# Shared expert's rows kept in SBUF and added in the last stage of a one-core encoder layer

## The reference

```
idx, wts = route(h2, w_router, router_bias)
shared = (jax.nn.silu(h2 @ w_sg) * (h2 @ w_su)) @ w_sd
ffn = routed_experts(h2, idx, wts, w_eg, w_eu, w_ed) + shared
x = layer_norm(ALPHA * x + ffn.reshape(B, T, D_MODEL), ln2_g, ln2_b)
```

## Time and profile before

| what | us |
|---|---|
| median of 3 runs | 2419.66 |
| lowest, highest run | 2417.68, 2421.93 |
| profiled execution, its own time | 2428.82 |
| its span, first to last instruction | 2426.9 |
| PE busy | 2284.9 (94%) |
| DVE busy | 1405.8 (58%) |
| ACT busy | 963.1 (40%) |
| POOL busy | 1496.5 (62%) |
| mean granted clock of TensorE | 0.987 |

### The profile page before, as it was taken

How to read it: one execution, slowest core, us unless ns; L and a number is a source line. 1 busy time by engine, 2 the same in 40 slices (tenths; PEclk the granted TensorE clock), 3 DMA queues, 4 the chain that set the end, 5 groups by cost and what they waited for, 6 DMA issues and landing times. The chain is left out here.

```text
span 2426.9 us, 40519 instructions
## 1 busy us (share of the span) xinstructions
PE 2284.9 (94%) x15460; PEld 2011.2 (83%) x15460; DVE 1405.8 (58%) x2749; ACT 963.1 (40%) x1582; POOL 1496.5 (62%) x1525
## 2 busy tenths in 40 slices
PE   4999999999999999999998999999999999999882
PEld 4889899898898998989987776578898888888882
DVE  7365665755756647557567697534455555555344
ACT  3452734526436346263364232122323333333334
POOL 6355674675646646657467256577667777776533
PEclk9999999999999999999998999999999999999996
DMA  5201112011011111111112641599999999999995
GB/s 181 77 28 45 41 45 60 29 44 50 29 45 49 46 50 37 36 50 37 47 38 78 194 133 47 154 281 300 310 348 350 354 352 350 351 352 360 363 353 181
DMA packets 210602, 380.72 MB, mean 157 GB/s; under 512 B 25810, under 2 KB 132558, under 8 KB 209898
## 3 DMA queue, kind: packets, MB, share of 16 engines
q1 hardware_dynamic: 180218, 302.25, 34.8%
q0 software_dynamic: 30192, 75.89, 13.1%
HBM read 310.71 MB, written 76.41 MB: 160 GB/s over the span
## 5 line engine op out<-in xcount | busy, mean ns | idle before, releaser
L128 PE MATMUL ps<-xTh,w_mix_low 128*128 128x368 f32 (+1 forms) x1728 | 594.1, 344 | 7.0 <-POOL w_mix_low L122 5.7
L130 PE MATMUL ps<-xTh,w_mix_high 128*128 128x368 f32 (+3 forms) x1808 | 598.9, 331 | 0.4 <-issue 0.4
L129 PE MATMUL ps<-xTl,w_mix_high 128*128 128x368 f32 (+3 forms) x1808 | 597.1, 330 | 1.5 <-issue 1.5
L2298 POOL DMA_INDIRECT xg_early<-h_d,tabq_early x304 | 313.2, 1030 | 153.8 <-issue 80.8
L129 PEld LDWEIGHTS ps<-xTl,w_mix_high 128*128 128x128 f32 (+1 forms) x1808 | 340.1, 188 | 15.8 <-issue 9.5
L128 PEld LDWEIGHTS ps<-xTh,w_mix_low 128*128 128x128 f32 x1728 | 329.3, 191 | 20.5 <-issue 15.4
L130 PEld LDWEIGHTS ps<-xTh,w_mix_high 128*128 128x128 f32 (+1 forms) x1808 | 339.4, 188 | 5.6 <-issue 1.8
L2310 POOL DMA_INDIRECT ys_d<-yo,tab_early x114 | 216.6, 1900 | 112.6 <-issue 50.6
L122 POOL TENSOR_TENSOR w_mix_low<-w_mix_raw,w_mix_high 128x1024 fp32r<-128x1024 f32 x72 | 182.7, 2537 | 120.9 <-ACT w_mix_high L117 83.1
L1333 POOL TENSOR_TENSOR x_m<-x_m,kh_m 128x128 f32<-128x128 f32 (+1 forms) x272 | 125.4, 461 | 114.6 <-ACT x_m L866 114.6
L2340 PEld LDWEIGHTS ps<-xgT,wg_early 128*128 128x128 f32 x1376 | 177.6, 190 | 19.3 <-issue 18.6
(11 more groups left out here) (396 smaller groups left out, 4558.8 us busy)
## 6 DMA issues: line engine op xcount, KB each, us to landing
wd_early<-in_w_exp_down SPq DMA_DIRECT2D x43, 1024.0 KB
wg_early<-in_w_exp_gate SPq DMA_DIRECT2D x82, 512.0 KB
wu_early<-in_w_exp_up SPq DMA_DIRECT2D x82, 512.0 KB
w_mix_raw<-in_w_in SPq DMA_DIRECT2D x72, 512.0 KB, 3.8
wg<-in_w_exp_gate SPq DMA_DIRECT2D x42, 512.0 KB
wu<-in_w_exp_up SPq DMA_DIRECT2D x42, 512.0 KB
wd<-in_w_exp_down SPq DMA_DIRECT2D x21, 1024.0 KB
xg_early<-h_d,tabq_early POOLq DMA_INDIRECT x316
```

Source lines behind the costliest of these rows:

```text
L128: pe.matmul(out, ll, rh, start=start, stop=False)
L129: pe.matmul(out, lh, rl, start=False, stop=False)
L130: return pe.matmul(out, lh, rh, start=False, stop=stop)
L2298: pool.indirect_dma_start(out=xg[:, b, g, :], out_offset=None, in_=h2_d[:, :].rearrange("t (q n) -> (t q) n", q=4), in_offset=bass.Indirec ...
```

## The change

The four buffers and the nine accumulating transfers go. All nine tiles of shared rows stay in one SBUF tensor, `shr`, to the end. To make room, tensors of the bridge that die early lie inside it: the shared expert's gate and up weights in tiles 2 to 5, gain and shift of the first norm in tiles 6 and 7, router weights and small tables in tile 8. `rows_out` waits for these users at tiles 6 and 8 (for tiles 2 to 5 the order of TensorE's queue does it). The planes of expert 62 lie in the dead second buffers of gate and up weights, expert 63 uses `wdh` and `wdl`. In the last stage each loaded tile first gets its shared rows added (a join), four on VectorE and five on GpSimd, and ScalarE's measures wait for GpSimd's joins. `last_norm` now loads into `yn`, which lies over buffers of the experts. The name `LATE`, defined twice before (65536, then 6), is split in two: `BEHIND` takes the second meaning and `LATE` keeps 65536 for rows past an expert's room.

```diff
@@ bridge
-        wg, wu, wd = sb("swg", [P, KT, FE]), sb("swu", [P, KT, FE]), sb("swd", [P, 2, D])
-        hT, sl, ys = sb("shT", [P, 2, T]), sb("ssl", [P, 2, 368]), sb("ys", [P, 2, D])
+        wd = sb("swd", [P, 2, D])
+        shr = sb("shr", [P, NT, D])
+        wg, wu = (shr[:, t:t + 2, :].rearrange("p t d -> p (t d)").rearrange("p (k n) -> p k n", k=KT) for t in (2, 4))
+        gcol, bcol = shr[:, 6, :], shr[:, 7, :]
+        wr, rb = shr[:, 8, 0:KT * NE].rearrange("p (k n) -> p k n", k=KT), shr[:, 8, KT * NE:(KT + 1) * NE]
+        hT, sl = sb("shT", [P, 2, T]), sb("ssl", [P, 2, 368])
...
                 act.wait_ge(d_done, 2 * t + b + 1)
-                if b == 0 and t == 2:
-                    act.wait_ge(m_low, NT - 1)
-                if b == 0 and t >= 4:
-                    act.wait_ge(y_out[t % 4], 16 * (t // 4))
-                act.activation(shared_rows(t)[:m, cols(b)], ps[:m, (G, U)[b], :], ACT.Copy, scale=1.0 / ALPHA).then_inc((y_left, y_right)[b], 1)
+                if b == 0 and t == 6:
+                    act.wait_ge(y_ready, NT)
+                if b == 0 and t == 8:
+                    act.wait_ge(routed, NT)
+                act.activation(shr[:m, t, cols(b)], ps[:m, (G, U)[b], :], ACT.Copy, scale=1.0 / ALPHA).then_inc((y_left, y_right)[b], 1)
...
-            def add_shared(t):
-                m = rows(t)
-                pool.wait_ge(y_left, t + 1)
-                pool.wait_ge(y_right, t + 1)
-                pool.wait_ge(stored[t % 2], 32 * (t // 2 + 1))
-                pool.dma_start(ys_d[t * P:t * P + m, :], shared_rows(t)[:m, :], accum_op=ALU.add).then_inc(y_out[t % 4], 16)
-
...
-            add_shared(0)
-            add_shared(1)
-            add_shared(2)
-            add_shared(3)
-            add_shared(4)
             gather(0)
-            add_shared(5)
             gather(1)
-            add_shared(6)
-            add_shared(7)
-            add_shared(8)
@@ experts
-            n = e - (NE - 2)
-            return (wdh[:, :, :], wdl[:, :, :]) if n < 0 else (last_planes[:, n, 0, :, :], last_planes[:, n, 1, :, :])
+            return (last_high[:, :, :], last_low[:, :, :]) if e == NE - 2 else (wdh[:, :, :], wdl[:, :, :])
...
-            for n in range(4):
-                pool.wait_ge(y_out[n], 16 * len(range(n, NT, 4)))
...
-                if e and e < NE - 2:
+                if e == NE - 2:
+                    act.wait_ge(u_done, e)
+                elif e == NE - 1:
+                    act.wait_ge(d_done, e - 1)
+                elif e:
                     act.wait_ge(d_done, e)
@@ last_norm, VectorE's measure, ScalarE's measure, GpSimd
             dve.wait_ge(y_in[t], 16)
+            dve.tensor_tensor(xr[:m, t, :], xr[:m, t, :], shr[:m, t, :], ALU.add).then_inc(joined, 1)
+            dve.wait_ge(joined, n + 1)
...
-            act.wait_ge(y_in[t], 16)
+            act.wait_ge(joined_pool, n + 1)
...
+        def join(t):
+            m = rows(t)
+            pool.wait_ge(y_in[t], 16)
+            pool.tensor_tensor(xr[:m, t, :], xr[:m, t, :], shr[:m, t, :], ALU.add).then_inc(joined_pool, 1)
+
+        join(MEASURED[0])
+        join(MEASURED[1])
         pool.wait_ge(rows_in, 32)
         for n, t in enumerate(BY_POOL):
             m = rows(t)
+            join(MEASURED[n + 2])
             pool.wait_ge(unit_ready, n + 1)
```

More of the change, by code:

```diff
@@ L180, in first_experts @@
                 ("tab", [P, NE, 2], U32), ("tabw", [P, NE, 2], F32), ("tb", [NE, CAP, 2], U32), ("tbf", [NE, CAP], F32),
-                ("twice", [NE, 2, LOW], F32), ("fourfold", [NE, 4, QUAD], F32), ("tabq", [P, GROUPS, NE], U32))]
+                ("twice", [NE, 2, LOW], F32), ("fourfold", [NE, 4, QUAD], F32), ("tabq", [P, GROUPS, NE], U32))[begin:]]
         constants(nc, ident, ones, before)
@@ L202, in build @@
             ns, nb, nl = (len(x.split()) for x in (SHARED_SEMAPHORES, BRIDGE_SEMAPHORES, LAST_SEMAPHORES))
-            bridge(nc, block, sems[:ns], sems[ns:ns + nb], a, ps, ident, ones, before, st, w_raw, w_high, late, woh, wol, mT_d, xn_d, h2_d, ys_d, tok_d, plan_d,
+            shr = bridge(nc, block, sems[:ns], sems[ns:ns + nb], a, ps, ident, ones, before, st, w_raw, w_high, late, woh, wol, mT_d, xn_d, h2_d, ys_d, tok_d, plan_d,
                    gates_d, only_d, dest_d, picks_d, pairs_d, step_d, limit_d, place, order, early)
@@ L206, in build @@
             c2 = ctx.enter_context(ExitStack())
-            first_experts(c2, "_reserved")
+            last_planes = []
+            for n in ("high", "low"):
+                c2.enter_context(nc.sbuf_tensor("first_of_two_" + n, [P, KT, FE], F32))
+                last_planes.append(c2.enter_context(nc.sbuf_tensor("last_" + n, [P, 2, D], F32R)))
+            first_experts(c2, "_reserved", 2)
             wg, wu, wd, xg, tab, tabw, tabq = early[:6] + early[-1:]
-            bufs = [wg, wu, wd, xg] + [c2.enter_context(nc.sbuf_tensor(n, shape, F32)) for n, shape in (
-                ("sl", [P, 2 * CAP]), ("yo", [P, 2, 2, D]))]
-            last, added = experts(nc, block, sems[:ns], sems[ns + nb:-nl], a, ps, ident, h2_d, ys_d, order, tab, tabw, tabq, bufs, c2)
+            bufs = [wg, wu, wd, xg]
+            last, added = experts(nc, block, sems[:ns], sems[ns + nb:-nl], a, ps, ident, h2_d, ys_d, order, tab, tabw, tabq, shr, last_planes, bufs, c2)
             last_norm(nc, block, sems[-nl:], a, o, ps, ys_d, added, *last)
@@ L1258, in _ @@
                 last_merge()
-                for k in range(EARLY, LATE):
+                for k in range(EARLY, BEHIND):
                     dve.wait_ge(wo_high, k + 1)
@@ L1443, in bridge @@
         only = sb("only", [P, NE])
-        fill = sb("fill", [P, 2 * FILL], U32)
+        fill = shr[:, 8, (KT + 2) * NE:(KT + 2) * NE + 2 * FILL].bitcast(U32)
         tokens = sb("tokens", [P, NT], U32)
@@ L1553, in first_tile @@
                 for k in range(FIRST, HEADS):
-                    if k >= LATE:
-                        pe.wait_ge(wo_low, k - LATE + 1)
+                    if k >= BEHIND:
+                        pe.wait_ge(wo_low, k - BEHIND + 1)
                     for b in range(2):
@@ L1910, in tables @@
                     dve.tensor_copy(tabw[:, some, j], ps[:, RB, n * NE:(n + 1) * NE][:, some]).then_inc(tab_s, 1)
-            for k in range(LATE, HEADS):
-                split_low(dve, wol[:, k, :], late[k - LATE], woh[:, k, :]).then_inc(wo_low, 1)
+            for k in range(BEHIND, HEADS):
+                split_low(dve, wol[:, k, :], late[k - BEHIND], woh[:, k, :]).then_inc(wo_low, 1)
             dve.wait_ge(first_high, 1)
@@ L2184, in _, with experts @@
             send(8)
-            add_shared(0)
-            add_shared(1)
-            add_shared(2)
-            add_shared(3)
-            add_shared(4)
             gather(0)
-            add_shared(5)
             gather(1)
-            add_shared(6)
-            add_shared(7)
-            add_shared(8)
-def experts(nc, block, both, sems, a, ps, ident, h2_d, ys_d, order, tab, tabw, tabq, bufs, stack):
-    wg, wu, wd, xg, sl, yo = bufs
+        return shr
+def experts(nc, block, both, sems, a, ps, ident, h2_d, ys_d, order, tab, tabw, tabq, shr, last_planes, bufs, stack):
+    wg, wu, wd, xg = bufs
+    last_high, last_low = last_planes
     second = [cap - P for cap in PLACE_CAP]
```

60 lines of the change are left out of this document (30 added, 30 removed).

## The result

Median 2424.10 us over 20 runs (2421.38 to 2427.73), against 2417.99 us over 20 runs of the kernel before (2416.36 to 2422.39). The ratio is 1.0021, 95% interval 1.0014 to 1.0028: slower, by 6.1 us between the medians, about 5 us by the ratio. The forecast was 2424.2 from a base of 2419.7, so the time was met and the difference was forecast 1.6 us too small.

The account below looks back on a forecast made before the run. The expert loop was taken to start bound by TensorE and end bound by transfers. Start -3.3 and last stage +7.8 gave +4.5 us on 2419.7, so 2424.2 us, range 2419.7 to 2428.5.

Parts of the forecast that it names:

- Part 1: Bridge's end: without the nine accumulating transfers ScalarE no longer waits, so TensorE starts expert 0 3.3 us earlier.
- Part 2: Gathers for expert 0: the sixth lands in 3.8 us, its rows turned 1.2 us ahead of TensorE.
- Rival C: Bridge's end: expert 0's gathers land as late as before, the start's whole gain is lost; +7.8 us, chance 0.12.
- Part 3: Expert loop: loads follow TensorE's progress, so the whole loop moves by the same 3.3 us.
- Parts 4 and 5: Planes of the last two experts and new eviction waits of tiles 6 and 8: already met, 0 us each.
- Parts 6 to 8: Last stage: VectorE's four joins, GpSimd's five, and their mutual exclusion; the last store is issued 7.8 us later.
- rival B: Last stage: VectorE and GpSimd don't hold each other up, some 2.9 us less; +1.6 us in all, chance 0.14.
- the last store is issued 7.8 us later: End of last stage: both engines' chains end at 2429, the last two stores fall together; +7.8 us.
- Rival E: Expert loop: transfers bound it from the first expert, so the nine transfers' time comes back; say -8 us, chance 0.07.

Follow-up runs that it names:

- the longer kernel before: The kernel before the change, with 109 empty instructions ahead of GpSimd's loop over the experts; 2421.02 us, ratio 1.0012.

## Why the prediction was right in its number, and where it was not

The range held the result, but that the time was met to 0.1 us is luck. The base was 1.7 us too high (2419.7 from three runs, 2418.0 from twenty). What the sum covers, the span, grew by about 3 us by its medians, where 4.5 were forecast; the tail, which it left as it was, grew by 3.15. Slower by over 0.2% had 0.43, within 0.2% had 0.50; the ratio of 1.0021 lies on the border. Term by term:

- *Part 1, ScalarE's waits go, 3.3 us.* The size was right: with the weights held back the start came 3.7 us earlier. The cause was not. The buffers alone gave nothing (19.96); what counted was that the transfers stood in the way of the gathers. The price of a late start was also read from a trace in which the clock stayed up; in two others the first product took 1.7 and 2.9 us longer besides.
- *Part 2, the gathers land in 3.8 us and don't bind.* This step failed. They took 5.59 us (5.0 to 5.6 in the like runs) and did bind: TensorE stood still for 1.90 us, 0.73 of which the last eviction would have cost anyway. The row used as nearest was a plain load on an idle queue; here 2 MB of weights were under way. Without these they take 2.2 us. The gain fell from the 3.3 us forecast to 2.5. Rival C had the threshold (5 us) and the reason right, but priced it as all or nothing; a landing between the two gives a part.
- *Part 3, the experts' loop shifts as a whole.* It does: 803.4 and 803.9 us in the two traces.
- *Parts 4 and 5, planes and new waits at 0.* Nothing in the loop's length speaks against it; it was not tested by itself.
- *Parts 6 to 8, the last stage, +7.8.* Up to the last operation it was +6.5. The joins took 7.43 us in sum (2.15, 2.16, 1.54 and 1.58) where 8.4 were forecast, and both engines did end together. The hold-up is worth 2.0 us of the stage by the run with PSUM operands (rival B put it at 2.9). The term that was too large is the waiting: 3.5 us were put in, and the joins took 7.43 - 4.9 = 2.5 us more than by themselves. Leaving out GpSimd's joins alone shortened the stage by only 0.3 us, since VectorE's chain stays.
- *What was missing: the end.* The step "the last store is issued 7.8 us later" took the rest of the program as unchanged. It grew by 2.1 us in the span and by 2.3 (3.15 in the medians) behind it. The latter is shown to hang on the length of GpSimd's program. Of the former, some 1.3 us is that GpSimd no longer ends ahead of VectorE; the other 0.9 is not explained.
- *Rival E* (transfers bound the loop from the first expert, so that taking 4.5 MB out gains 8 us) did not happen, yet the two runs that put them into the loop lost 13.7 and 25. The loop had nothing to gain from fewer transfers at its start, and no room for more later on. The working of this rival has a slip: 4.5 MB at 132 GB/s are 34 us and not 20, so its lower end would have been -26 and not -12.

**Open.** The stretches of the two traces add to +8.9 us, the medians say 6.1. Most of the gap is the clock at the start. The experts' part was 803.4, 804.7 and 806.9 us in the three traces with the transfers in the bridge, and 802.8 to 804.3 in the eight without any; the slower first product is 1.7 of the 804.7 and 2.9 of the 806.9, and less these all three lie within the eight. From the slot product to the span's end it is 859.7 us in the longer kernel before and 863.4 in the changed one: with the 3.15 us of the tails that makes 6.9. How often the kernel before loses its clock there is not known, since only one trace of it and one of its longer form are kept. Not settled is the distance from GpSimd's last operation to the span's end. It is 7.5 us in all eight kernels without accumulating transfers of the shared rows, 6.6 to 6.7 where those are in the bridge or right behind it, and 8.4 where they are spread, whatever the program's length. Why nineteen instructions decide about the tail is shown only as far as the packet behind the span goes.

No correct version beat the kernel before. The run with no joins, which leaves work out, came to 0.9991, but with the longer tail. By its median span and a tail of 1.8 us it would be at 2413.4, some 5 us under the kernel before; that is an estimate, not run. So the transfers in the bridge do cost something, 4.4 us by the median spans with and without them (2416.0 and 2411.6). The joins cost more (7.6 us by spans, 2419.2 and 2411.6), and so did the transfers in every other place that was tried.

## What to carry to other kernels

Price a transfer by what is in flight when it lands: the last of the same six gathers landed after 2.2 us with no weights in flight, after 5.0 to 5.6 beside weights, and after 7.6 to 8.0 beside weights and accumulating transfers. When an engine is to wait less, look also at how fast it ran behind the wait: here the clock made a wait of 4 us cost up to 2.9 us more. Before work is moved out of a stage with idle transfer time, look for the DMA share of the stage where it would go, and for the engine time at the program's end, where every microsecond counts in full. When a change adds or takes away instructions, compare own time and span first: here 2.6 of 6.1 us hung on the length of one engine's program and came back with 19 empty instructions. And when two engines hold each other up, work taken from one of them gives little: leaving out GpSimd's five joins gave 1.2 us, VectorE's four 0.7, both 8.0, the first two within the noise.

## What the runs showed of the hardware

- **The place of the code.** With GpSimd's program at 2610, 2620 or 2748 instructions one more piece of code was fetched some 3 to 4 us behind the span's end, and the execution lasted 2.6 to 3.4 us longer behind its span than at 2637 to 2653. 2620 and 2748 lie 128 apart and behave alike. The Trainium skill (Runtime: NRT & Kernel Launch, "Instruction fetch mechanics") says that a taken branch whose target isn't in the fetched window forces a fetch before execution goes on; the packet behind the span agrees with it, and this program ends with a branch on every engine; whether its target lies outside the window no run here shows. The same section gives blocks of 256 instructions; the runs can't tell 128 from 256.
- **Mutual exclusion is tied to the operand, not to the operation.** The same VectorE addition took 1.22 us with one operand in PSUM and up to 2.74 with both in SBUF beside GpSimd, and GpSimd's 2.35 became 3.2 to 3.3.
- **The clock behind a wait.** TensorE's first expert product took 5.44 us at a granted clock of 1.00, and 7.12 and 8.33 us in the two traces in which it came behind 4.42 and 4.06 us of standing still and the clock was 0.50 for 3.4 and 6.8 us around its start. Where it stood still for 2.75 and 1.45, or for 1.90, the clock stayed at 1.00.
